# Low halves of the weights written over the raw ones, in one ring of four slots

## What is computed

```python
for l in range(DEPTH):
    sh1, sc1, g1, sh2, sc2, g2 = adaln(cond, w_ada[l], b_ada[l])
    h = rmsnorm(x, norm_g[l, 0]) * (1 + sc1) + sh1
    y = na(h, w_qkv_na, w_o_na) if l % 2 == 0 else gla(h, w_qkvg_gla, w_o_gla)
    x = x + g1 * rmsnorm(y, norm_g[l, 1])
    h = rmsnorm(x, norm_g[l, 2]) * (1 + sc2) + sh2
    x = x + g2 * rmsnorm(square(relu(h @ w1_mlp[l])) @ w2_mlp[l], norm_g[l, 3])
```

## Time and profile before

| | before |
|---|---|
| median of the runs | 2565.05 us (2562.69 to 2568.68, three runs) |
| span of the profiled execution | 2568.2 us (no other time is listed for it) |
| PE busy | 2506.8 us, 98% |
| PE loading weights | 2018.0 us, 79% |
| DVE busy | 1368.2 us, 53% |
| ACT busy | 1050.6 us, 41% |
| POOL busy | 114.6 us, 4% |
| data moved | 634.51 MB, mean 247 GB/s |

### The profile page before, as it was taken

How to read it: one execution, slowest core, us unless ns; L and a number is a source line. 1 busy time by engine, 2 the same in 40 slices (tenths; PEclk the granted TensorE clock), 3 DMA queues, 4 the chain that set the end, 5 groups by cost and what they waited for, 6 DMA issues and landing times.

```text
span 2568.2 us, 37169 instructions
## 1 busy us (share of the span) xinstructions
PE 2506.8 (98%) x14658; PEld 2018.0 (79%) x14658; DVE 1368.2 (53%) x1492; ACT 1050.6 (41%) x1148; POOL 114.6 (4%) x164
## 2 busy tenths in 40 slices
PE   6899999989999999999999999999999999999998
PEld 3578888778778778778887777797787888888887
DVE  2244544475445445545565454565755564565565
ACT  3223334364333333333353365584633333343342
POOL 0020000000000000000000023200000000000000
PEclk8999999999999999999999999999999999999999
DMA  9989888958888887887867954458588555555554
GB/s 360 356 263 298 281 289 283 353 179 284 293 267 268 283 298 251 273 301 236 284 238 255 315 172 164 158 191 282 185 260 287 170 193 199 169 191 198 187 197 173
DMA packets 493365, 634.51 MB, mean 247 GB/s; under 512 B 12128, under 2 KB 370320, under 8 KB 491984
## 3 DMA queue, kind: packets, MB, share of 16 engines
q1 hardware_dynamic: 484576, 608.46, 70.9%
q0 software_dynamic: 6352, 23.31, 2.7%
q10 hardware_dynamic: 2336, 1.31, 0.2%
HBM read 623.90 MB, written 9.13 MB: 246 GB/s over the span
## 4 chain that ended last, share of the span: by engine, by line
PE 79%; DMA 9%; DVE 5%; ACT 4%; issue 2%; SPq 0%; ACTq 0%; DVEq 0%
PE PS L1295 24%; PE PS L1296 12%; PE PS L1363 10%; PE PS L1364 10%; PE PS L1365 10%; PE PS L1322 5%; DVE WLO L1856 3%; DMA RAW<-in_w_qkvg_gla 3%; ACT WHI L1600 2%; DMA RAW<-in_w_o_na 2%; DMA RAW<-in_w_o_gla 2%; DMA SCR<-in_w_ada 1%; DMA RAW<-in_w_mlp 1%; PE PS L1476 1%; PE PS L1501 1%
## 5 line engine op out<-in xcount | busy, mean ns | idle before, releaser
L1856 DVE TENSOR_TENSOR WLO<-RAW,WHI 128x2048 fp32r<-128x2048 f32 x384 | 878.3, 2299 | 756.7 <-ACT WHI L1600 747.6
L1600 ACT ACTIVATE WHI<-RAW 128x2048 fp32r<-128x2048 f32 x384 | 730.5, 1913 | 725.8 <-DMA RAW<-in_w_mlp 474.5
L1295 PE MATMUL PS<-HM,WHI 128*128 128x512 f32 x2560 | 914.7, 401 | 7.8 <-DVE SCR L2094 5.0
L1296 PE MATMUL PS<-HM,WLO 128*128 128x256 f32 x2560 | 719.2, 281 | 0.0
L1295 PEld LDWEIGHTS PS<-HM,WHI 128*128 128x128 f32 x2560 | 482.4, 188 | 139.7 <-issue 17.3
L1296 PEld LDWEIGHTS PS<-HM,WLO 128*128 128x128 f32 x2560 | 484.8, 189 | 0.2
L1363 PE MATMUL PS<-WHI,HID 128*128 128x512 f32 x1152 | 453.9, 394 | 5.0 <-DVE WLO L1856 5.0
L1364 PE MATMUL PS<-WLO,HID 128*128 128x512 f32 x1152 | 449.5, 390 | 0.0
L1365 PE MATMUL PS<-WHI,HID 128*128 128x512 f32 x1152 | 449.0, 390 | 0.0
L1363 PEld LDWEIGHTS PS<-WHI,HID 128*128 128x128 f32 x1152 | 216.7, 188 | 62.8 <-issue 17.5
L1365 PEld LDWEIGHTS PS<-WHI,HID 128*128 128x128 f32 x1152 | 216.8, 188 | 45.7
(11 more groups left out here) (239 smaller groups left out, 1731.5 us busy)
## 6 DMA issues: line engine op xcount, KB each, us to landing
RAW<-in_w_mlp SPq DMA_DIRECT2D x256, 1024.0 KB, 6.1
ADW<-in_w_ada SPq DMA_DIRECT2D x176, 1024.0 KB, 8.1
RAW<-in_w_qkv_na SPq DMA_DIRECT2D x48, 1024.0 KB, 6.9
RAW<-in_w_qkvg_gla SPq DMA_DIRECT2D x32, 1024.0 KB, 7.2
SCR<-in_w_ada SPq DMA_DIRECT2D x16, 1024.0 KB, 11.5
RAW<-in_w_o_na SPq DMA_DIRECT2D x16, 1024.0 KB, 7.1
RAW<-in_w_qkvg_gla SPq DMA_DIRECT2D x32, 512.0 KB, 4.7
RAW<-in_w_o_gla SPq DMA_DIRECT2D x16, 1024.0 KB, 6.5
```

Source lines behind the costliest of these rows:

```text
L1295: mm(bank[:, 0:2 * T2], hi[:, k, cols], act[:, kc, 0:2 * T2], start=first, stop=False)
L1296: return mm(bank[:, 0:T2], lo[:, k, cols], act[:, kc, 0:T2], start=False, stop=last)
L1600: actv(WHI[:, 2 * s + u, 0:n], RAW[:, u, 0:n], ACT.Copy).then_inc(hi_done, 1)
L1856: tt(WLO[:, 2 * s + u, 0:n], RAW[:, u, 0:n], WHI[:, 2 * s + u, 0:n].bitcast(f32), ALU.subtract).then_inc(lo_done, 1)
```

## The change

`WLO` becomes a second name of `RAW`: RAW has four slots, slot 2*s+u, and DVE writes the low half over the raw unit in place. A slot is free for the next load when PE is done with the low half in it, so the load of unit k waits for PE to be done with unit k - 4 (`slot_free`), and no longer for DVE. The copy on ACT no longer waits for PE. The semaphores of arrival are four instead of two. In the first stage the places of the loads of units 5 to 11 in SP's list move: units 4 to 11 stood behind (3,2), (3,3), (4,1), (4,3), (5,2), (6,0), (7,3), (7,3), and stand behind (3,2), (4,0), (4,2), (5,2), (6,0), (6,2), (7,2), (7,3); the splits of units 5 and 8 move later in the lists of ACT and DVE. The number and shape of DMAs, copies, subtractions and matmuls stay as they are. 16 KB per partition of SBUF are no longer taken.

```diff
     pass
 TMP = sb("TMP", [P, 2 * KC * T2])
 X = sb("X", [P, 2, D])
-RAW = sb("RAW", [P, 2, UNIT])
+with nc.sbuf_tensor("WLO", [P, 4, UNIT], f32r) as WLO:
+    pass
+RAW = sb("RAW", [P, 4, UNIT])
 WHI = sb("WHI", [P, 4, UNIT], f32r)
-WLO = sb("WLO", [P, 4, UNIT], f32r)
 ADW = sb("ADW", [P, 2, UNIT])
 CB = sb("CB", [P, 2048])
 BASE = sb("BASE", [P, P + 2])
...
-raw_in = [sem("raw_in0"), sem("raw_in1")]
-key_in = [sem("key_in0"), sem("key_in1")]
+raw_in = [sem(f"raw_in{slot}") for slot in range(4)]
+key_in = [sem(f"key_in{slot}") for slot in range(4)]
...
 @block.sync
 def _(sp):
-    def load_slab(m, w, row, col):
+    def slot_free(m, u):
+
+        if u == 0:
+            sp.wait_ge(unit0_used, m + 1)
+        else:
+            sp.wait_ge(block_done, m * 2 + 2)
+
+    def load_slab(m, s, w, row, col):
         for u in range(2):
-            sp.wait_ge(lo_done, m * 2 + u + 1)
+            slot = 2 * s + u
+            slot_free(m, u)
             src = w[ds(row + u * UNIT_ROWS, UNIT_ROWS), ds(col, UC)].rearrange("(c p) n -> p c n", p=P)
-            sp.dma_start(RAW[:, u, :].rearrange("p (c n) -> p c n", c=UKC), src).then_inc(raw_in[u], 16)
+            sp.dma_start(RAW[:, slot, :].rearrange("p (c n) -> p c n", c=UKC), src).then_inc(raw_in[slot], 16)
     def load_ada(a, layer, col):
...
-                load_slab(i * 2 + (m + s), w, row, i * (2 * UC) + s * UC)
+                load_slab(i * 2 + (m + s), s, w, row, i * (2 * UC) + s * UC)
-            sp.wait_ge(lo_done, m0 * 2 + (4 * n + x + 1))
+            slot_free(m0 + (2 * n + x // 2), x % 2)
-            sp.dma_start(RAW[:, x % 2, :].rearrange("p (c n) -> p c n", c=4), src).then_inc(raw_in[x % 2], 16)
+            sp.dma_start(RAW[:, x, :].rearrange("p (c n) -> p c n", c=4), src).then_inc(raw_in[x], 16)
...
     def load_first_weights(q):
-        j, v, u = q // FV, q % FV, q % 2
+        j, v, slot = q // FV, q % FV, q % 4
         col = 2 * D + FC * v
-        sp.wait_ge(lo_done, M_QKV0 * 2 + q + 1)
+        slot_free(M_QKV0 + q // 2, q % 2)
         src = wq0[FC * j:FC * j + FC, col:col + FC].rearrange("(c p) n -> p c n", p=P)
-        sp.dma_start(RAW[:, u, :].rearrange("p (c n) -> p c n", c=FG), src).then_inc(raw_in[u], 16)
-
-    sp.sem_inc(raw_in[0], 16 * M_QKV0)
-    sp.sem_inc(raw_in[1], 16 * M_QKV0)
+        sp.dma_start(RAW[:, slot, :].rearrange("p (c n) -> p c n", c=FG), src).then_inc(raw_in[slot], 16)
+
+    for slot in range(4):
+        sp.sem_inc(raw_in[slot], 8 * M_QKV0)
     sp.dma_start(BASE[:, :], t_base).then_inc(sem("small_in"), 16)
     sp.dma_start(SMALL[:, 0, :], norm_g.rearrange("l j (c p) -> (l j c) p", p=P)).then_inc(
         sem("small_in"), 16)
...
-    first_weights = {(0, 3): (0, 1), (2, 1): (2,), (2, 3): (3,), (3, 2): (4,), (3, 3): (5,), (4, 1): (6,),
-                     (4, 3): (7,), (5, 2): (8,), (6, 0): (9,), (7, 3): (10, 11)}
+    first_weights = {(0, 3): (0, 1), (2, 1): (2,), (2, 3): (3,), (3, 2): (4,), (4, 0): (5,), (4, 2): (6,),
+                     (5, 2): (7,), (6, 0): (8,), (6, 2): (9,), (7, 2): (10,), (7, 3): (11,)}
...
-            sp.wait_ge(lo_done, (M_QKV1 + R_QK) * 2 + (4 * h + x + 1))
-            dst = RAW[:, x % 2, :].rearrange("p (c n) -> p c n", c=4)
+            slot_free(M_QKV1 + R_QK + 2 * h + x // 2, x % 2)
+            dst = RAW[:, x, :].rearrange("p (c n) -> p c n", c=4)
...
     def split_hi(m, s, n=UNIT, units=range(2), keys=0):
         for u in units:
-            act.wait_ge(raw_in[u], m * 16 + 16)
+            slot = 2 * s + u
+            act.wait_ge(raw_in[slot], (m - s) * 8 + 16)
             if keys:
-                act.wait_ge(key_in[u], keys * 16)
-            if u == 0:
-                act.wait_ge(unit0_used, m + 1)
-            else:
-                act.wait_ge(block_done, m * 2 + 2)
-            actv(WHI[:, 2 * s + u, 0:n], RAW[:, u, 0:n], ACT.Copy).then_inc(hi_done, 1)
+                act.wait_ge(key_in[slot], (keys + 1) // 2 * 16)
+            actv(WHI[:, slot, 0:n], RAW[:, slot, 0:n], ACT.Copy).then_inc(hi_done, 1)
     def ada_row(a, first=False, bank=ROWB):
         act.wait_ge(ada_done, a + 2)
...
-    first_splits = {0: (0, 1), 2: (4, 5), 4: (7, 8), 6: (9,)}
-    late_splits = {0: (2, 3), 1: (6,), 3: (10, 11)}
+    first_splits = {0: (0, 1), 2: (4,), 4: (7,), 6: (9,)}
+    late_splits = {0: (2, 3), 1: (5, 6), 2: (8,), 3: (10, 11)}
...
     def split_lo(m, s, n=UNIT, units=range(2)):
         for u in units:
             dve.wait_ge(hi_done, m * 2 + u + 1)
-            tt(WLO[:, 2 * s + u, 0:n], RAW[:, u, 0:n], WHI[:, 2 * s + u, 0:n].bitcast(f32),
+            slot = 2 * s + u
+            tt(WLO[:, slot, 0:n], RAW[:, slot, 0:n], WHI[:, slot, 0:n].bitcast(f32),
                ALU.subtract).then_inc(lo_done, 1)
     def sum_rows(i):
...
-        for q in {0: (0, 1), 1: (4, 5), 2: (7, 8), 3: (9,)}[j]:
+        for q in {0: (0, 1), 1: (4,), 2: (7,), 3: (9,)}[j]:
-        for q in {0: (2, 3), 1: (6,), 2: (), 3: (10, 11)}[j]:
+        for q in {0: (2, 3), 1: (5, 6), 2: (8,), 3: (10, 11)}[j]:
```

More of the change, by code:

```diff
@@ L1174, in na_column @@
                 return "QKV".index(kind) * D + j * UC
-            load_slab(M_REST, wq0, 0, na_column(*ORDER[0]))
+            load_slab(M_REST, M_REST % 2, wq0, 0, na_column(*ORDER[0]))
             sp.wait_ge(first_used, 4 * 7 + 2)
@@ L1179, in _ @@
             for r in range(1, SLABS):
-                load_slab(M_REST + r, wq0, 0, na_column(*ORDER[r]))
+                load_slab(M_REST + r, (M_REST + r) % 2, wq0, 0, na_column(*ORDER[r]))
                 load_ada(A_QKV0 + r, 0, (A_QKV0 + r) * UC)
@@ L1202, in mlp_group @@
                     for s in range(2):
-                        load_slab(g * (4 * NB) + i * 2 + (m + s), w1_mlp[layer], 0, g * D + i * (2 * UC) + s * UC)
+                        load_slab(g * (4 * NB) + i * 2 + (m + s), s, w1_mlp[layer], 0, g * D + i * (2 * UC) + s * UC)
                         if s == 0:
@@ L1228, in _ @@
                             "(c p) n -> p c n", p=P)
-                        sp.dma_start(dst[:, :, DK * j:DK * j + DK], src).then_inc(arrived[x % 2], 16)
+                        sp.dma_start(dst[:, :, DK * j:DK * j + DK], src).then_inc(arrived[x], 16)
             for n in range(len(GATE_INCS)):
@@ L1233, in _ @@
                 for s in range(2):
-                    load_slab(i * 2 + (M_QKV1 + R_G + s), wq1, 0, i * (2 * UC) + (2 * KEY + D + s * UC))
+                    load_slab(i * 2 + (M_QKV1 + R_G + s), s, wq1, 0, i * (2 * UC) + (2 * KEY + D + s * UC))
             sp.wait_ge(sem("gla_o"), ITEMS)
```

## The result

| | before | after |
|---|---|---|
| median of the timed runs | 2565.74 us (4 runs) | 2596.70 us (2592.04 to 2603.27, 4 runs) |
| ratio | | 1.0119, interval 1.0107 to 1.0131 |
| span of the profiled execution | 2568.2 us | 2601.5 us |
| PE busy | 2506.8 us | 2516.2 us |
| mean granted clock | 0.991 | 0.989 |

The change costs 31 us: slower, as forecast, by twice the size (forecast 15.6), and outside the range of 2562 to 2592.

A forecast was written before the change was run, and what follows sets the result against it. The prediction took PE, busy 2506.8 of 2568.2 us, as the bound. Its terms, -5.5 + 11.6 + 6.0 + 3.5 = +15.6 us on a median of 2565.05, gave 2580.6, stated as 2580, range 2562 to 2592.

The forecast's parts named there:

- The bound, and the steady stretches: PE bounds the kernel; both MLPs, the first mixer's projections and the DMA-bound output product change by zero.
- the rival of weights: In steady stretches PE waits for weights landing late behind adaLN loads: 26 us more, 2607; chance 0.06.
- The rival that only the start matters: Earlier issue gains 6.6 us at unit 12 and 4.0 at the output product, losses absorbed: 2554.4 us; chance 0.07.
- that of no difference: Half of the delays in GLA, between stages and in last slabs vanish in slack: 2562 to 2570 us; chance 0.17.
- Part 1, the start: First stage: unit 12's load goes out earlier, ahead of POOL's bias loads; a gain of 5.5 us, ends 0 to 6.6.
- Part 2, GLA: GLA's first item, four odd items and tail: ACT stands before copies whose loads wait for PE; a loss of 11.6 us.
- Part 3, between the stages: At three stage ends the last evacuation waits behind the next stage's splits; a loss of 6.0 us, ends 3 and 9.
- Part 4, the last slabs: Last slabs of both MLPs and GLA: units wanted after 2.72 us come late; a loss of 3.5 us, ends 1 and 6.

The follow-up runs named there:

- small_store: Changed kernel with GpSimd's stores of GLA's final state cut to 16 of 128 partitions; 2598.47 us, ratio 1.012 to the kernel before.
- before_pad: Kernel before with three more exponentials on ACT ahead of each odd GLA item's decays; 2574.77 us, ratio 1.0028.
- stage_order: Changed kernel with the split of the next stage's second unit moved behind the norm at stage ends; 2593.52 us, ratio 1.0105 to the kernel before.
- before_wait2: Kernel before, own buffers, where slab numbers are constant loads also wait for PE to finish unit k - 4; 2607.95 us, ratio 1.0157.
- gla_order: Changed kernel with copy and subtraction of each GLA slab's second unit moved behind the item's activations; 2581.34 us, ratio 1.0053 to the kernel before.

## Why the prediction was half right

**The bound, and the steady stretches: right.** The two MLPs have the same length between their first and last slabs; no repeated wait for L1863 shows, and the rival of weights falls. The rival that only the start matters and that of no difference fall with the +31 us.

**Part 1, the start: right.** The load goes out at 142.76, the subtraction takes 2.29 us, the addition on GpSimd comes after it, and PE starts unit 12 at 158.88 (near 160 was forecast):

```profile
142.76 5.81 SPq L1115 DMA_DIRECT2D RAW<-in_w_qkv_na  x2
...
150.45 2.29 DVE L1863 TENSOR_TENSOR WLO<-RAW,WHI 128x2048 fp32r<-128x2048 f32 x1 [3.95 <-ACT WHI L1606]
...
154.80 4.62 POOL L2202 TENSOR_TENSOR CB<-CB,WINM 128x2048 f32<-128x2048 f32 x1 [8.10 <-DMA CB<-rpb_pad]
...
158.88 0.39 PE L1304 MATMUL PS<-HM,WHI 128*128 128x512 f32 x1
```

6.2 were won up to there, 1.0 of it in the first stage, and 1.55 by unit 12 running at full pace. Units 15 to 18 gave back 2.7: the loads there, `w_ada` and weights, landed in 12 to 15 us, and PE waited once for `w_ada`; the rest of the 2.7 I can't place.

```profile
PE PS L1331 <- DMA ADW<-in_w_ada: 1.4, 1, 1.4
```

The sum is the forecast's by errors that cancel, which is luck.

**Part 2, GLA: the mechanism right, its price half of what it was.** This is the step that failed. The first item (2.16 against 2.1), two of the odd items (2.16 and 1.64 against 1.55) and the tail (3.6 against 3.3) came as worked out. Missing were a term for the clock, 6.8 us behind four of the five waits, and a landing time other than the shortest: I took 5.0 us for all, though the earlier trace rows showed a median of 7.0 in another stretch, and two loads of 6.5 and 7.2 us cost 4.8. The high end of the part, 17.4, all but reached what the items and the tail lost by themselves (17.5, about 1.1 of it slower matmuls within the items), but had no room for the 6.8 behind them. The 24.3 of GLA against 11.6 are 12.7 of the 17.7 us by which the sum of 15.6 fell short of 33.3. (The forecast also set the span of 2568.2 beside the median of the times; the time of every run that lists both is about 1.8 us above its span, so that execution was some 4.9 us above the median and not 3.2. The sum does not hang on it.)

**Part 3, between the stages: right place, right size at two of three.** The evacuation waits for the subtraction at all three, here at the end of the first MLP:

```profile
1351.58 2.29 DVE L1863 TENSOR_TENSOR WLO<-RAW,WHI 128x2048 fp32r<-128x2048 f32 x1
1353.78 0.69 DVE L1949 TENSOR_TENSOR SCR<-PS,SCR 128x512 f32<-128x512 f32 x1
```

This evacuation stood at 1351.27 before, 2.51 earlier, of which the stage before it accounts for 0.16. At the end of the attention the gap grew by 3.27, but the unit behind it ran at full pace where it had not before (5.53 instead of 7.17 us), and a further 0.1 us per unit over 14 units came back, which I can't explain. A longer gap does not always cost its length.

**Part 4, the last slabs: one term mis-sized.** The first MLP lost 4.25 where 0.85 was forecast:

```profile
1330.90 0.47 PE L1372 MATMUL PS<-WHI,HID 128*128 128x512 f32 x1 [3.28 <-DVE WLO L1863]
```

I had credited the `w_ada` loads in the same queue as cover; here the delay went through in full (0.67 before, 3.28 now), and behind it the clock was 0.76 for 1.6 us more, which small_store with the same wait was spared. The other two (2.2 against 1.3, 1.6 against 1.35) are near. The output product of the attention, taken as zero, lost 0.9.

## What to carry to other kernels

When a buffer's release moves from an engine that finishes early to the one that finishes last, the full landing time enters every in-order list in which the next split stands: look at what stands behind that split, and move it in front, before judging the saved buffer; here that gave back two thirds of the loss, and the new order of the last slab the rest. Price a new wait of TensorE with the landing times of its own stretch, not the shortest, and add a range for what the matmuls behind it may take at the lower clock. And a wait put into a queue that also carries other loads delays those: the list of the loads has to change with the rule that frees their slots.

## What the runs showed of the hardware

- Waits of PE of 1.4 to 1.9 us went both ways. Behind those of 1.42 and 1.86 in the changed kernel, 1.45 in before_pad, 1.51 and 1.56 in stage_order, 1.58 in before_wait2 and 1.84 in gla_order the granted clock was 1.00; behind 1.58 in the changed kernel, 1.47 in small_store and 1.71 in before_wait2 it was 0.84 to 0.85 in the next 11 us. Every wait of 2.2 to 3.8 us in GLA was followed by slower matmuls (0.73 to 0.83 in the windows shown), but one of 3.31 in a last slab was not. The slower matmuls behind an item cost 1.2 to 2.6 us, and up to 1.9 more within it.
- A load that runs alone in GLA lands in 5.0 to 5.1 us, but units 221 and 229 needed 6.5 and 7.2 in the same place of their items, 6.0 and 6.4 with the stores cut, and in stage_order 6.7 and 5.1.
- The subtraction of 2048 columns took 2.29 us where GpSimd was idle and 4.71 beside its addition; the change moved them apart.
